# Stacked half-precision sample-state products and an earlier chunk-state scan in a hybrid decoder step on one core

## The reference

```python
def hgrn2_block(s0, q, k, v, log_f):
    b = jnp.cumsum(log_f, axis=1)
    ...
    o = jnp.einsum('bhts,bshv->bthv', scores, v) + jnp.einsum('bthk,bhkv->bthv', q * jnp.exp(b), s0)
    b_last = b[:, -1]
    s_new = jnp.exp(b_last)[..., None] * s0 + jnp.einsum('bshk,bshv->bhkv', k * jnp.exp(b_last[:, None] - b), v)
    return s_new, o

def retention_block(s0, q, k, v):
    ...
    s_new = jnp.exp(c * log_gamma)[None, :, None, None] * s0 + jnp.einsum('bshk,bshv->bhkv', k * k_dec[None, :, :, None], v)
    return s_new, o
```

## Time and profile before

| | before |
|---|---|
| median of 3 runs | 1737.02 us (1736.96 to 1738.49) |
| profiled execution | 1742.57 us, span of the trace 1741.0 us |
| PE busy | 1567.8 us (90%) |
| DVE busy | 904.5 us (52%) |
| ACT busy | 654.0 us (38%) |
| POOL busy | 154.3 us (9%) |
| mixer of layer 0, of layer 1 in the trace | about 49 to 420 us, 892 to 1263 us |
| mean granted TensorE clock | 0.931 |

### The profile page before, as it was taken

How to read it: one execution, slowest core, us unless ns; L and a number is a source line. 1 busy time by engine, 2 the same in 40 slices (tenths; PEclk the granted TensorE clock), 3 DMA queues, 4 the chain that set the end, 5 groups by cost and what they waited for, 6 DMA issues and landing times.

```text
span 1741.0 us, 31399 instructions
## 1 busy us (share of the span) xinstructions
PE 1567.8 (90%) x12107; PEld 1251.0 (72%) x12107; DVE 904.5 (52%) x1389; ACT 654.0 (38%) x920; POOL 154.3 (9%) x126
## 2 busy tenths in 40 slices
PE   4699999989699999999867999999886999999994
PEld 3477777767578888788755777777765888887883
DVE  4766644444565555533266665444356555553334
ACT  3645523332353334422155452333225443333213
POOL 2111111100200000000030111000002000000002
PEclk8799989988899999999978899999888999999997
DMA  6132222221123332233221224232031223322321
GB/s 192 46 90 77 75 75 75 74 74 55 57 73 97 96 96 77 70 93 95 82 66 51 74 74 111 57 88 78 27 97 48 88 83 96 96 81 74 97 66 51
DMA packets 175035, 138.05 MB, mean 79 GB/s; under 512 B 5064, under 2 KB 169192, under 8 KB 174776
## 3 DMA queue, kind: packets, MB, share of 16 engines
q1 hardware_dynamic: 168192, 113.46, 22.0%
q0 software_dynamic: 5408, 18.60, 3.8%
q10 hardware_dynamic: 1372, 5.16, 0.9%
HBM read 125.12 MB, written 12.07 MB: 79 GB/s over the span
## 4 chain that ended last, share of the span: by engine, by line
PE 77%; DVE 9%; ACT 6%; issue 4%; DVEq 2%; ACTq 1%; DMA 1%; SPq 0%
PE ACC L510 61%; PE SCR L624 2%; PE OT L632 2%; PE SCR L662 1%; ACT WH L830 1%; DVE X L1193 1%; PE OT L684 1%; PE SCR L545 1%; PE SCR L727 1%; DVE Z L1222 1%; DVE Fb L1206 1%; DVE WL L1153 1%; PE OT L600 1%; DVEq L1261 1%; PE OT L599 1%
## 5 line engine op out<-in xcount | busy, mean ns | idle before, releaser
L510 PE MATMUL ACC<-XH,WH 128*128 128x280 f16 x2432 | 502.6, 289 | 70.8 <-DVE XL L1196 43.1
L510 PE MATMUL ACC<-XL,WH 128*128 128x280 f16 x2432 | 502.4, 289 | 0.0
L510 PE MATMUL ACC<-XH,WL 128*128 128x280 f16 x2432 | 501.6, 289 | 0.0
L510 PEld LDWEIGHTS ACC<-XH,WH 128*128 128x128 f16 x2432 | 238.7, 101 | 153.0 <-DVE XL L1196 45.6
L1153 DVE SCALAR_TENSOR_TENSOR WL<-stage,WH 128x2048 f16<-128x2048 f32 (+1 forms) x116 | 245.9, 2120 | 182.0 <-ACT WH L830 170.2
L510 PEld LDWEIGHTS ACC<-XL,WH 128*128 128x128 f16 x2432 | 243.3, 100 | 58.6
L510 PEld LDWEIGHTS ACC<-XH,WL 128*128 128x128 f16 x2432 | 243.3, 100 | 58.0
L830 ACT ACTIVATE WH<-stage 128x2048 f16<-128x2048 f32 (+1 forms) x116 | 204.8, 1766 | 103.7 <-PE ACC L510 86.9
L510 PE MATMUL ACC<-shared,WH 128*128 128x280 f16 x1408 | 225.2, 283 | 0.2
L510 PEld LDWEIGHTS ACC<-shared,WH 128*128 128x128 f16 x1408 | 137.6, 98 | 30.8 <-issue 0.8
L510 PE MATMUL ACC<-shared,WL 128*128 128x280 f16 x704 | 141.5, 283 | 0.0
(11 more groups left out here) (238 smaller groups left out, 1791.4 us busy)
## 6 DMA issues: line engine op xcount, KB each, us to landing
stage<-in_w_in_dram SPq DMA_DIRECT2D x64, 512.0 KB, 5.3
stage<-in_w_a_dram SPq DMA_DIRECT2D x44, 512.0 KB, 4.3
stage<-in_w_b_dram SPq DMA_DIRECT2D x44, 512.0 KB, 4.8
stage<-in_w_down_dram SPq DMA_DIRECT2D x32, 384.0 KB, 3.3
stage<-in_w_down_dram SPq DMA_DIRECT2D x32, 320.0 KB, 3.7
out_dram<-shared POOLq DMA_DIRECT2D x16, 512.0 KB, 3.9
stage<-in_w_o_dram SPq DMA_DIRECT2D x16, 512.0 KB, 3.9
shared<-in_state_hgrn_dram POOLq DMA_DIRECT2D x8, 512.0 KB, 5.7
```

The lines of the kernel that those rows point to most:

```text
L510: last = mm(ACC[:, acc, h, 0:HALF], lhs, x[:, xk + k, h * HALF:(h + 1) * HALF], start=begin, stop=end)
```

## The change

Three edits.

1. **Stacked half-precision sample states.** The 32 sample tokens are laid out three times, 96 rows. For the keys these rows are high, high and low half, for the values high, low and high half, so that one f16 product over 96 rows is the sum of the three partial products. DVE repeats the key columns (`twice(KE)`) and ACT repeats the value columns out of the accumulator (`twice(V)`) so that the transposes give 96 rows. ACT writes these rows twice: `KV3` in f16 and `KVF` in f32. DVE subtracts to get the two low parts (`low_sample_rows`) and signals the new semaphore `kv_low`, on which POOL now waits instead of `tok_ready`. `VX` is f16 with 96 rows. `low_sample_rows` stands on DVE behind the first gate instruction in groups 1 to 3, ahead of `rt_key` in group 4, and at the end of `rt_a` for the retention heads.
2. **Chunk states ahead of the exponent differences** on DVE in groups 1 to 3.
3. **ACT reads the query accumulator ahead of the decay exponentials** in groups 1 to 3 too.

```diff
-        VX = sb("VX", [TS, DEC_BATCH, P])
-        KVTS = sb("KVTS", [TS, 2, P])
+        VX = sb("VX", [TS3, DEC_BATCH, P], F16)
+        KV3 = sb("KV3", [TS3, 2, P], F16)
+        KVF = sb("KVF", [TS3, 2, P])
...
+        def twice(t):
+            return t[:, T:T + 2 * TS].rearrange("p (a t) -> p a t", a=2)
...
-                pool.wait_ge(tok_ready, hh + 1)
-                nc.gpsimd.tensor_tensor(VX[:, :, :], KVTS[:, 1:2, :].to_broadcast([TS, DEC_BATCH, P]), bcast(seqm[0:TS, :], P),
+                pool.wait_ge(kv_low, hh + 1)
+                nc.gpsimd.tensor_tensor(VX[:, :, :], KV3[:, 1:2, :].to_broadcast([TS3, DEC_BATCH, P]), bcast(seqm[0:TS3, :], P),
...
-                            last = nc.tensor.transpose(SCR[0:TS, bank, i * P:(i + 1) * P], src[:, TP:T], ident)
+                            last = nc.tensor.transpose(SCR[0:TS3, bank, i * P:(i + 1) * P], src[:, TP:TP + TS3], ident)
...
-                mm(SCR[:, bank, :], KVTS[:, 0, :], VX[:, 4 * n:4 * n + 4, :].rearrange("p b v -> p (b v)"),
+                mm(SCR[:, bank, :], KV3[:, 0, :], VX[:, 4 * n:4 * n + 4, :].rearrange("p b v -> p (b v)"),
...
-                f(halves(buf[:, 0:T]), ACC[:, c, :, 0:HALF], ACT.Copy, scale=INV_W).then_inc(acc_read[c], 1)
+                last = f(halves(buf[:, 0:T]), ACC[:, c, :, 0:HALF], ACT.Copy, scale=INV_W)
+                if buf is V:
+                    last = f(twice(V), ACC[:, c, 1:2, HALF - TS:HALF].to_broadcast([P, 2, TS]), ACT.Copy, scale=INV_W)
+                last.then_inc(acc_read[c], 1)
...
-                f(KVTS[:, :, :], SCR[0:TS, 0, 0:2 * P].rearrange("p (n v) -> p n v", n=2), ACT.Copy).then_inc(scr_read[0], 1)
+                f(KV3[:, :, :], SCR[0:TS3, 0, 0:2 * P].rearrange("p (n v) -> p n v", n=2), ACT.Copy)
+                f(KVF[:, :, :], SCR[0:TS3, 0, 0:2 * P].rearrange("p (n v) -> p n v", n=2), ACT.Copy).then_inc(scr_read[0], 1)
...
-                f(KVTS[:, 0, :], SCR[0:TS, 0, 2 * P:3 * P], ACT.Copy, scale=tab[0:TS, ds(cols["k_dec_s"][0] + p, 1)])
-                f(KVTS[:, 1, :], SCR[0:TS, 0, 3 * P:4 * P], ACT.Copy).then_inc(scr_read[0], 1)
+                for rows_ in (KV3, KVF):
+                    f(rows_[:, 0, :], SCR[0:TS3, 0, 2 * P:3 * P], ACT.Copy, scale=tab[0:TS3, ds(cols["k_dec_s"][0] + p, 1)])
+                    last = f(rows_[:, 1, :], SCR[0:TS3, 0, 3 * P:4 * P], ACT.Copy)
+                last.then_inc(scr_read[0], 1)
...
-                    if d is None:
-                        read_acc(Q, 1, tile + 1, None)
+                    read_acc(Q, 1, tile + 1, None)
                     hg_exponentials(l, head)
-                    if d is not None:
-                        read_acc(Q, 1, tile + 1, None)
...
+            def low_sample_rows(hh):
+                dve.wait_ge(tok_ready, hh + 1)
+                for n, rows_ in enumerate((slice(2 * TS, TS3), slice(TS, 2 * TS))):
+                    tt(KV3[rows_, n, :], KVF[rows_, n, :], KV3[rows_, n, :], ALU.subtract)
+                dve.drain().then_inc(kv_low, 1)
...
                 tt(QD[:, 0:T], Q[:, 0:T], E[:, 0:T], ALU.mult)
+                nc.vector.tensor_copy(twice(KE), KE[:, TP:T].unsqueeze(1).to_broadcast([P, 2, TS]))
...
                 dve.drain().then_inc(pts_ready, 1)
+                low_sample_rows(hh)
...
                 if kind == 0:
-                    hg_gate(l, head, tile)
-                    hg_exponents(l, head)
+                    hg_gate(l, head, tile, hgrn_rows)
                     if b is not None:
                         b()
+                    hg_exponents(l, head)
```

More of the change, by code:

```diff
@@ L46 @@
 T = TP + TS
+TS3 = 3 * TS
 HALF = T // 2
@@ L143, in const_tables @@
     put("mask32", causal)
-    put("seq", tok[:, None] // DEC_SEQ == np.arange(DEC_BATCH)[None, :])
+    put("seq", np.tile(tok[:, None] // DEC_SEQ == np.arange(DEC_BATCH)[None, :], (3, 1)))
     log_g = np.log1p(-np.exp2(-5.0 - np.arange(HEADS)))
@@ L154, in const_tables @@
     put("k_dec", np.where(left >= 0, np.exp(np.maximum(left, 0) * log_g[None, None, :]), 0.0) * root)
-    put("k_dec_s", np.exp((DEC_SEQ - 1 - tok % DEC_SEQ)[:, None] * log_g[None, :]) * root)
+    put("k_dec_s", np.tile(np.exp((DEC_SEQ - 1 - tok % DEC_SEQ)[:, None] * log_g[None, :]) * root, (3, 1)))
     put("gamma4", np.broadcast_to(np.exp(DEC_SEQ * log_g), (P, HEADS)))
@@ L218, in hybrid_decoder_step @@
         Fb, T1, T2, T3, B, Q, QS, QD, KE, E, V, G = (
-            sb(n, [P, T + 2]) for n in ("Fb", "T1", "T2", "T3", "B", "Q", "QS", "QD", "KE", "E", "V", "G"))
+            sb(n, [P, T + (2 * TS if n in ("KE", "V") else 2)]) for n in ("Fb", "T1", "T2", "T3", "B", "Q", "QS", "QD", "KE", "E", "V", "G"))
         at = [0]
@@ L291, in hybrid_decoder_step @@
         tok_ready, vx_ready, pts_ready, states_ready = sem("tok_ready"), sem("vx_ready"), sem("pts_ready"), sem("states_ready")
+        kv_low = sem("kv_low")
         decays_used = sem("decays_used")
@@ L629, in sample_output @@
                 cols_ = OT[:, 1, TP - SPLIT:REST]
-                mm(cols_, KVTS[:, 1, :], PTSS[:, :], start=True, stop=False, skip_group_check=True)
+                mm(cols_, KVF[0:TS, 1, :], PTSS[:, :], start=True, stop=False, skip_group_check=True)
                 for b in range(DEC_BATCH):
@@ L653, in rest_transposes @@
                         nc.tensor.transpose(SCR[0:TAIL, 0, n * P:(n + 1) * P], src[:, 4 * P:TP], ident)
-                        last = nc.tensor.transpose(SCR[0:TS, 0, (2 + n) * P:(3 + n) * P], src[:, TP:T], ident)
+                        last = nc.tensor.transpose(SCR[0:TS3, 0, (2 + n) * P:(3 + n) * P], src[:, TP:TP + TS3], ident)
                     last.then_inc(scr_full, 1)
@@ L1196, in norm_apply, with hg_gate @@
                         tt(XL[:, m - 2, :], X[:, m - 2, :], XH[:, m - 2, :], ALU.subtract).then_inc(x_ready, 1)
-            def hg_gate(l, p, tile):
+            def low_sample_rows(hh):
[3 more added lines that the diff above has]
+                dve.drain().then_inc(kv_low, 1)
+            def hg_gate(l, p, tile, low_rows=None):
                 n = l * HEADS + p
@@ L1203, in hg_gate @@
                 dve.drain().then_inc(f_ready, 1)
+                if low_rows is not None:
+                    low_rows()
                 dve.wait_ge(lnf_parts, n + 1)
@@ L1436, in group @@
                 split_lo(1, j)
+                hgrn_rows = (lambda: low_sample_rows(hh - 1)) if steps else None
                 if kind == 0:
-                    hg_gate(l, head, tile)
-                    hg_exponents(l, head)
+                    hg_gate(l, head, tile, hgrn_rows)
                     if b is not None:
                         b()
+                    hg_exponents(l, head)
                     if d is not None:
@@ L1446, in group @@
                     if after_hgrn:
+                        hgrn_rows()
                         dve.wait_ge(tok_ready, hh)
```

## The result

The changed kernel takes **1747.59 us** (median of 5 runs, 1745.30 to 1748.68), the kernel before in the same session 1737.02 (1736.96 to 1739.26): ratio 1.0051, 95% interval 1.0038 to 1.0065. It is slower by about 10 us, on the side that the forecast leaned to, and 7.6 us above its time.

The account below looks back on a forecast made before the run. PE, 90% busy, was read as the bound, losing some 5 of 41.2 us in a loop group. Terms +6.1, -2.9, -1.2 and +0.4 summed to +2.4 us, carried to the median: forecast 1740 us, range 1713 to 1757.

Parts of the forecast that it names:

- at slot 28 for ACT's squares: HGRN2 loop groups: PE, some 5 us faster, would wait here for squares behind the late query sigmoid, about 3.5 us.
- the 2.0 us of room: HGRN2 loop groups: the slack read in the ring per group, against which 3.55 us of added work was set.
- the ring: Dependency chain between loop groups, from PE's slot 3 through DVE and ACT to the next slot 3; predicted +1.55 us a group.
- the 3.55 of the sum: Lengthening of the ring per loop group: low rows 1.0, chunk states 2.9, query read -0.5, key repeat 0.15 us.
- (b): HGRN2 loop groups: the ring has more room than read, PE stays the bound, -4.5 us each; 1706 us, chance 0.12.
- Group 4: One a layer, no exponentials: wait grows to 2.3 us, products save 2.25; -1.45 us each, -2.9 in all.
- Retention: Six loop heads: products -1.6, copy +0.41, `VX` +0.55, rotation +0.35, key repeat +0.1; -0.2 us each, -1.2 in all.
- The exposed second copy: Retention heads: ACT's second pair of copies holds the bank the next score product takes, +0.41 us.
- The sum: Whole kernel: HGRN2 loops +6.1, group 4 -2.9, retention -1.2, last retention heads +0.4; +2.4 us on the profiled 1742.57.
- (a): Retention heads: DVE's low split goes ahead of `VX`, +2.0 us to each of eight heads; 1755 us, chance 0.15.
- (c): POOL: f16 `VX` much shorter, 0.95 us instead of 1.89; 1726 us (1751 if 2.8 us), chance 0.22.
- (d): HGRN2 loop groups: lower clock falls into slots 4 to 10, 1.7 us times six; 1750 us, chance 0.13.

Follow-up runs that it names:

- run 1: The changed kernel with the chunk states put back behind the exponent differences; stacked products and early query read stay: 1731.47 us, 0.9952 of before.
- run 4: The changed kernel with DVE's sample-state add moved ahead of its wait for the exponentials: 1730.75 us, 0.9958 of before.
- run 10: The changed kernel with the sample-state add ahead of the wait for the exponentials and GpSimd's decay product ahead of `VX`: 1711.96 us, 0.9848 of before.
- run 2: Stacking alone: the changed kernel with chunk states back behind the differences and query read back behind the exponentials: 1730.94 us, 0.9943 of before.
- run 3: The kernel before with the two moves of order alone (chunk states, query read), nothing stacked: 1748.93 us, 1.0064 of before.
- run 9: The kernel before with GpSimd's decay product of the sample states ahead of `VX`, nothing else: 1715.62 us, 0.9870 of before.
- run 7: The changed kernel with a retention head's low rows subtracted between the third and fourth group of score copies: 1739.37 us, 1.0006 of before.
- run 5: The kernel of run 1 with GpSimd's decay product of the sample states ahead of `VX` in the HGRN2 heads: 1704.29 us, 0.9803 of before.

## Why the prediction came out as it did

**The step that failed** is the one on where PE waits in the loop groups: "at slot 28 for ACT's squares", and at slot 3. It waits at slot 28 for DVE, and at no slot 3. The prediction followed the exponentials through DVE to `QD` and left out that the sample add, which frees PE's scratch bank, stands in that queue. In the old order this add is done before slot 28 (run 1, DVE and PE); in the new one it is not.

```profile
162.08 1.27 DVE L1321 TENSOR_TENSOR shared<-shared,SCR 128x512 f32<-128x512 f32 x2
```

```profile
165.19 1.11 PE L616 MATMUL SCR<-shared,tab 128*128 128x264 f32 x4
```

With this step fell the 2.0 us of room that the ring was to give back. From a steady gate to `QD` DVE takes 25.74 us instead of 22.50, 3.2 more, near the 3.55 of the sum; but from `QD` to the next gate it takes 18.67, as before (18.68). PE sets the length there: in the hand-over shown it starts slot 28 23.36 us after the gate and needs 21.05 from there to the next gate, at the lower clock at first, where before has 22.20 and 18.98. That is the whole 3.2 us of a group.

Run 4 takes the add out of this place, and the groups come to 41.8 to 43.0 us, 1.5 to 2.8 less. That is about the predicted 42.7, but by another sum: a group is 20.8 to 21.2 us up to slot 28 and 20.8 to 22.2 behind it, with the lower clock in all six, and PE waits at no slot 3. The estimate of 42.7 to 43.1 us in run 4, with the add back on DVE's way to `QD`, speaks for the ring and its +1.55 us; no run shows it. Waits at slot 3 came only in run 10.

**The ring's terms.** The low rows took 0.58 us (0.4 to 0.5 predicted), the repeat of the keys 0.19 (0.15), the early query read fell into idle time, and in the old order its 0.5 us lay in room (run 2), the gate add grew from 2.20 to 2.84. The chunk states ahead of the differences are the loss: 3.2 us of a steady group against run 1, and 2.6 to 3.1 on the kernel before in run 3.

**The saving on PE in the loop groups**, some 5 us in the prediction's first paragraph and 4.5 in its rival (b), was not PE's to keep even in the old order. Run 1: 41.26 us a steady group with stacked products, 41.18 without. PE's sample product is itself a link of a ring, from GpSimd's hold on the gate add through scan, differences and chunk states to PE and the next gate. The first paragraph of the prediction took the 2.45 us as the change's to remove; run 9 shows that most of it belonged to GpSimd's order.

**Group 4** was predicted at -1.45 each and came to -4.4. The wait is 2.42 us (2.3 predicted), the products 0.39 each. What was mis-sized is the clock: before, it stood at 0.50 from 231.3 to 238.1 us; after, it stays at 1.00 there. The prediction had named this case and priced it at 1.45 more; 6.8 us at half speed come to some 3.4 (an estimate). Part of this is given back behind `QD` of group 4, where the lower clock lasts from 250.9 to 257.7 us instead of 248.4 to 251.8: from PE's first score product of group 4 to that of group 5 it is 47.28 us instead of 50.19, 2.9 less in each layer.

**Retention**: -0.2 predicted, 40.76 to 40.55 measured between steady heads. The two terms on which it rests, 0.55 for `VX` and 0.35 for the rotation behind the split, are run 7: 0.87 us of 0.90, of which the timelines of PE put 0.53 ahead of the first sample product and 0.34 between it and the sample outputs. The exposed second copy was too large: PE's wait for it (L669) is 2.6 us in 8 times, 0.20 in a steady head, not 0.41.

**The sum.** The forecast was +2.4 us on the profiled execution, and the two profiled executions differ by +2.7. That nearness is luck: it comes from errors of opposite sign, +13.8 instead of +6.1 in the loop groups and -8.8 instead of -2.9 in group 4, with -2.5 instead of -0.8 in retention (where one head of each layer is 1.6 us longer in that execution of before). And the sum was carried to the median as it was. In the profiled execution of before the groups 1 of the two layers are 6.6 us longer than two steady groups; the sum took 3.2 of them as time to win, and the median of before, 5.55 below that execution, seems to hold less of them. No trace shows the median's own execution; but of the later executions of before those near 1743 us had a mean granted clock of 0.930, and those near 1735 of 0.938 to 0.939. The execution of after lies 2.3 below its median, and so the medians differ by 10.6 us.

**The rivals.** (a) did not come, by the margin that it named: GpSimd started `VX` at 314.93 us, DVE issued the split at 315.08, 0.15 later, and was held. (c) did not come: `VX` in f16 takes 1.887 us on average, the 1.89 of f32. (b) did not come: the groups got 3.2 us longer. (d) came in another place: the lower clock lay at slots 28 to 31, not at 4 to 10.

The rule of the Trainium skill's page "SBUF — State Buffer", section "Who interferes with whom", that a DVE instruction with two SBUF inputs and a GpSimd instruction that reads SBUF exclude each other, is borne out by four lengths of the same gate add: 0.74 us with none in the way, 0.97 behind the end of one, 2.20 behind one that had just begun, and 2.84 behind two. The trace agrees.

## What to carry to other kernels

When a step is moved ahead in one engine's queue, list every instruction that it is put in front of and ask of each which buffer or bank it frees: the one that hurt here was no link of the chain that was followed. Where a bound engine waits, follow the releaser back to the first instruction that is longer than its like elsewhere (a 0.74 us add that shows 2.20 us) before the work around the wait is made smaller; that cure was worth 24 us, two instructions in another order. And price a wait on PE with the clock behind it: 1.9 us of a shorter wait gave 3.45 us in a group.

## What the runs showed of the chip that was not expected

TensorE's clock behind the wait for the chunk states: in groups 2 and 3 it fell to 0.50 after waits of 2.45 us (before) and 3.37 (run 1), and not after 1.49 (run 5) or 0.99 (run 9). The length of the wait alone does not decide it, though. In group 1 it fell after 1.51 us in run 5 and after 1.01 in run 9. In group 4 it fell after 1.49 us in before (window of before):

```profile
231.50:238.00 6.50, 6.50 (x23) 3.38 (x22) 3.56 (x4) 1.91 (x1) 1.50 (x2) 0.50 0.10 33
```

and stayed at 1.00 after 2.42 us in the changed kernel (PE and a window):

```profile
238.72 0.39 PE L631 MATMUL SCR<-VX,KV 96*128 96x512 f16 x1 [2.42 <-DVE shared L1368]
```

```profile
239.00:250.00 11.00, 11.00 (x96) 9.60 (x94) 5.29 (x7) 2.36 (x3) 1.50 (x2) 1.00 0.52 146
```

Nor does it take a wait: in the retention heads of the changed kernel it falls with no idle time on PE just before, while the 16 sample output products of 4 columns each have ended 0.4 us earlier:

```profile
323.63 1.95 PE L639 MATMUL OT<-QS,shared 128*128 128x4 f32 x16
325.44 0.40 PE L517 MATMUL ACC<-XH,WH 128*128 128x280 f16 x2
...
325.91 0.62 PE L517 MATMUL ACC<-XH,WL 128*128 128x280 f16 x2
```

A head of before with the same products kept its clock (1.00 throughout the one from 288.18 to 328.94 us). What decides between these stays open. In these heads it cost nothing that could be seen: a head of run 4 without the slow stretch took 40.54 us, one of the changed kernel with it 40.55.
